# A two-layer decoder trunk: the first chunk fed from a transposed copy of x, and gate and up weights stored by chunk and row

## The reference, cut to what matters

```
def swiglu(x, w_gate, w_up, w_down):
    return (silu(x @ w_gate) * (x @ w_up)) @ w_down

for layer in range(2):
    x = x + 0.5 * swiglu(rmsnorm(x, ffn1_norm), ffn1_w_gate, ffn1_w_up, ffn1_w_down)
    h = rmsnorm(x, mix_norm)
    # h @ w_in gives q, k, v of three attention branches and three gate groups;
    # moba, sliding window with sinks, and differential attention with a headwise rmsnorm
    x = x + (sum of sigmoid(gate_i) * (branch_i @ P_i)) @ w_out
    x = x + 0.5 * swiglu(rmsnorm(x, ffn2_norm), ffn2_w_gate, ffn2_w_up, ffn2_w_down)
```

## Time and profile before

| | |
|---|---|
| time of the kernel, median of 3 runs | 1139.65 us (1139.65 to 1139.98) |
| time of the profiled execution | 1140.59 us |
| its span in the profile | 1138.8 us |
| PE busy | 1133.4 us |
| DVE busy | 770.4 us |
| ACT busy | 630.4 us |
| POOL busy | 70.3 us |
| read from memory | 205.29 MB |

### The profile page before, as it was taken

One profiled execution on the slowest core, in us unless ns is written; L12 is line 12 of the kernel. 1 busy time (PEld: TensorE's weight loads), 2 busy tenths in 40 slices (PEclk: granted clock), 3 DMA queues, 4 the chain that ended last, 5 costly groups with the idle time before them and its releaser, 6 DMA issues.

```text
span 1138.8 us, 16092 instructions
## 1 busy us (share of the span) xinstructions
PE 1133.4 (100%) x5975; PEld 966.9 (85%) x5975; DVE 770.4 (68%) x1055; ACT 630.4 (55%) x941; POOL 70.3 (6%) x79
## 2 busy tenths in 40 slices
PE   9999999999999999999999999999999999999999
PEld 7888888888888888888888888888888888888887
DVE  5766666868768676655766856678676695766655
ACT  6644455666684564544564544466666745544542
POOL 3020000202000000000020200002110000000000
PEclk9999999999999999999999999999999999999999
DMA  9955554545544665556566555636445445655521
GB/s 326 318 175 196 187 196 134 185 144 190 148 148 150 220 222 189 190 178 219 173 166 228 185 185 186 204 98 216 148 156 178 176 156 186 222 185 201 194 87 37
DMA packets 138828, 207.34 MB, mean 182 GB/s; under 512 B 6898, under 2 KB 99876, under 8 KB 138756
## 3 DMA queue, kind: packets, MB, share of 16 engines
q1 hardware_dynamic: 137364, 205.02, 54.5%
q0 software_dynamic: 752, 0.79, 0.7%
q10 hardware_dynamic: 640, 0.55, 0.2%
HBM read 205.29 MB, written 1.05 MB: 181 GB/s over the span
## 4 chain that ended last, share of the span: by engine, by line
PE 98%; ACT 1%; DVE 1%; issue 0%; DVEq 0%; ACTq 0%; POOL 0%; POOLq 0%
PE bank L560 28%; PE bank L530 16%; PE bank L534 16%; PE bank L533 16%; PE bank L564 15%; PE bank L546 1%; PE bank L859 1%; PE bank L849 1%; PE bank L830 1%; ACT probs L1202 1%; PE bank L848 1%; PE bank L877 1%; PE bank L668 0%; PE bank L569 0%; ACT w_high L1016 0%
## 5 line engine op out<-in xcount | busy, mean ns | idle before, releaser
L1300 DVE TENSOR_TENSOR w_low<-raw,w_high 128x1024 fp32r<-128x1024 f32 x388 | 464.2, 1232 | 282.1 <-ACT w_high L1016 281.4
L1016 ACT ACTIVATE w_high<-raw 128x1024 fp32r<-128x1024 f32 x387 | 393.6, 1055 | 318.4 <-PE bank L564 173.5
L560 PE MATMUL bank<-xT,w_high 128*128 128x512 f32 x1388 | 331.6, 390 | 0.1
L560 PEld LDWEIGHTS bank<-xT,w_high 128*128 128x128 f32 x1388 | 257.0, 188 | 51.2 <-DVE xT L1318 0.2
L564 PEld LDWEIGHTS bank<-xT,w_low 128*128 128x128 f32 x1408 | 175.7, 191 | 3.6
L564 PE MATMUL bank<-xT,w_low 128*128 128x256 f32 x1408 | 178.6, 283 | 0.0
L530 PE MATMUL bank<-w_high,xT 128*128 128x512 f32 (+1 forms) x440 | 171.3, 389 | 0.0
L534 PE MATMUL bank<-w_low,xT 128*128 128x512 f32 (+1 forms) x440 | 168.1, 382 | 0.0
L533 PE MATMUL bank<-w_high,xT 128*128 128x512 f32 (+1 forms) x440 | 168.1, 382 | 0.0
L530 PE MATMUL bank<-w_high,oT_high 128*128 128x512 f32 x418 | 162.6, 389 | 0.0
L534 PE MATMUL bank<-w_low,oT_high 128*128 128x512 f32 x418 | 162.2, 388 | 0.0
(11 more groups left out here) (146 smaller groups left out, 770.8 us busy)
## 6 DMA issues: line engine op xcount, KB each, us to landing
raw<-in_w_in SPq DMA_DIRECT2D x92, 512.0 KB, 4.5
raw<-in_ffn_w_down SPq DMA_DIRECT2D x88, 512.0 KB, 4.2
raw<-in_ffn_w_gate SPq DMA_DIRECT2D x86, 512.0 KB, 4.0
raw<-in_ffn_w_up SPq DMA_DIRECT2D x86, 512.0 KB, 5.0
raw<-in_w_out SPq DMA_DIRECT2D x16, 512.0 KB, 4.4
raw<-in_w_branch_c SPq DMA_DIRECT2D x8, 512.0 KB, 3.9
raw<-in_w_branch_a SPq DMA_DIRECT2D x4, 512.0 KB, 4.0
raw<-in_w_branch_b SPq DMA_DIRECT2D x4, 512.0 KB, 5.9
```

What stands on the lines that cost most here:

```text
L560: return nc.tensor.matmul(bank[b0 + n][:, :], w_high[:, slot, column(k, n)], xT[:, k], start=k == 0, stop=full_last and k == KB - 1)
L1016: act.activation(w_high[:, slot], raw[:, in_slot, (p % 2) * 1024:(p % 2) * 1024 + 1024], ACT.Copy).then_inc(sem["high_ready"], 1)
L1300: dve.tensor_tensor(w_low[:, slot], raw[:, FILL_SLOT[p // 2], (p % 2) * 1024:(p % 2) * 1024 + 1024], w_high[:, slot].bitcast(F32), ALU.sub ...
```

## The change

Three things are edited together.

1. **A transposed copy of x is an input.** The host passes `x_turned` (1024 x 256), `gains` (all gains and lam_init as columns, one transfer instead of four and some transposes), and x itself. The opening loads the transposed blocks in five pieces straight into SBUF (into the space of `o_nat`), so PE turns neither x nor the gains; ACT and DVE make the high and low blocks from SBUF. The first pair is split by its two row blocks: DVE itself copies the high half of block 0. ACT's squares of x are replaced by `sum_block_squares` on POOL, which squares the transposed x (two products of 128x1024) and adds the eight blocks together (sums of 1024, 512 and 256 columns); two matmuls with a column of ones (`sum_squares`) finish the sum over partitions. x in its normal layout is loaded later, by POOL's queue, and so are the parameters.
2. **Gate and up weights are laid out by chunk and row.** One array for gate and up together, so a fill of the ring is two transfers whose rows are 4 KB, and in the opening one transfer of 2 KB rows for each block, where both had 1 KB rows.
3. **Two numbers in the mixing part.** The first entries of `TURNS_AT` and `CONTEXTS_AT` go from 19 and 21 to 20 and 22.

On PE the turn of the norm's factor into a row (`turn_row`) moves: it stood between the wide passes of pairs 5 and 6, and stands after the narrow passes of pair 4; `sum_squares` takes its old place. The core of the diff:

```
-TURNS_AT = (19, 27, 35, 42)
-CONTEXTS_AT = (21, 29, 37, 44)
+TURNS_AT = (20, 27, 35, 42)
+CONTEXTS_AT = (22, 29, 37, 44)
...
-X_PIECES = (slice(0, 256), slice(256, 512), slice(512, 1024))
-WARM_FIRST, WARM_SECOND, WARM_THIRD = 6, 3, 6
+X_BLOCKS = ((0, 1), (1, 1), (2, 2), (4, 2), (6, 2))
+WARM = 11
...
+        def first_rows(engine, k0, nk, landed):
+            v = raw[:, FILL_SLOT[k0 // 4]].rearrange("p (k c) -> p k c", k=4)
+            for k in range(k0, k0 + nk):
+                engine.dma_start(v[:, k % 4], a["ffn1_gate_up"][0, 0, k // 4, :, k % 4]).then_inc(landed, 16)
...
+            def gate_up(w, layer, c, k0):
                 def sources(slot):
-                    v = slot.rearrange("p (k g c) -> p k g c", k=4, g=2)
-                    for g, w in enumerate((wg, wu)):
-                        yield v[:, :, g], w[bass.ds(layer, 1), k0 * P:(k0 + 4) * P, bass.ds(c * FC, FC)].rearrange(
-                            "o (k p) c -> p (o k) c", p=P)
+                    v = slot.rearrange("p (k c) -> p k c", k=4)
+                    for k in (0, 2):
+                        yield v[:, k:k + 2], w[bass.ds(layer, 1), bass.ds(c, 1), k0 // 4, :, k:k + 2].rearrange("o n p k c -> p (o n k) c")
...
+            load_x_turned(0)
+            load_x_turned(1)
+            load_x_turned(2)
+            first_rows(sp, 2, 2, fill_landed[FILL_SLOT[0]])
+            load_x_turned(3)
+            first_rows(sp, 4, 2, third_landed)
+            load_x_turned(4)
+            first_rows(sp, 6, 2, fill_landed[FILL_SLOT[1]])
...
+            def sum_block_squares():
+                for first, pieces in ((0, (0, 1, 2)), (D, (3, 4))):
+                    for piece in pieces:
+                        pool.wait_ge(x_turned_landed[piece], 16)
+                    v = x_turned[:, first:first + D]
+                    pool.tensor_tensor(x_squares[:, first:first + D], v, v, ALU.mult)
+                for width in (D, D // 2, D // 4):
+                    pool.drain()
+                    pool.tensor_tensor(x_squares[:, 0:width], x_squares[:, 0:width], x_squares[:, width:2 * width], ALU.add)
+                pool.drain().then_inc(block_squares_summed, 1)
...
+                pe.wait_ge(block0_high, 1)
                 pe.wait_ge(half_high, 1)
                 for n in range(4):
                     high_part(0, n, w_high, True)
+                pe.wait_ge(half_low, 1)
+                for n in range(4):
+                    high_part(0, n)
+                pe.wait_ge(block0_low, 1)
+                for n in range(4):
+                    low_part(0, n)
...
+            def cold_start():
+                act.wait_ge(gains_loaded, 16)
+                act.wait_ge(x_turned_landed[0], 16)
+                block(0).then_inc(block0_high, 1)
+                act.wait_ge(x_turned_landed[1], 16)
+                block(1).then_inc(sem["blocks_high"], 1)
                 high(0, 0)
+                for p in range(1, 4):
+                    act.wait_ge(x_turned_landed[p + 1], 16)
+                    block(2 * p)
+                    block(2 * p + 1).then_inc(sem["blocks_high"], 1)
+                    high(0, p)
                 high(0, 4)
...
+            def cold_pairs():
...
+                dve.wait_ge(half_landed[0], 16)
+                dve.tensor_copy(w_high[:, slot, 0:512], raw[:, in_slot, 0:512]).then_inc(half_high, 1)
+                dve.drain()
+                half_of_low(slice(0, 512)).then_inc(half_low, 1)
+                dve.wait_ge(block0_high, 1)
+                block_low(0).then_inc(block0_low, 1)
+                dve.wait_ge(sem["blocks_high"], 1)
+                block_low(1).then_inc(sem["blocks_low"], 1)
+                dve.wait_ge(sem["high_ready"], value("high_ready", 0, 1))
+                half_of_low(slice(512, 1024)).then_inc(sem["low_ready"], 1)
+                for p in range(1, 4):
+                    dve.wait_ge(sem["blocks_high"], p + 1)
+                    block_low(2 * p)
+                    block_low(2 * p + 1).then_inc(sem["blocks_low"], 1)
+                    low(0, p)
```

More of the change, by code:

```diff
@@ L506, in _ @@
                 pool.wait_ge(sem["hidden_ready"], value("hidden_ready", layer, 4))
+                if layer == 0:
+                    for half in range(HALVES):
+                        pool.dma_start(x[:, half], a["x"][0, half * P:half * P + P, :]).then_inc(x_loaded, 16)
                 pool.wait_ge(trig_loaded, 16)
@@ L667, in warm @@
                 for _ in range(count):
-                    nc.tensor.matmul(bank[7][:, :].rearrange("p (a b) -> p a b", a=4), zero[:, :],
-                                     zero[:, :].unsqueeze(1).to_broadcast([P, 4, P]), start=True, stop=True)
+                    nc.tensor.matmul(bank[7][:, :].rearrange("p (a b) -> p a b", a=4), ones[:, :],
+                                     ones[:, :].unsqueeze(1).to_broadcast([P, 4, P]), start=True, stop=True)
             def cold_chunk():
                 b0 = inner_bank(1)
[L675 to L680, removed]
                 full, high_part, low_part = inner_parts(PAIR_SLOT[0], b0)
-                pe.wait_ge(sem["blocks_high"], 1)
+                pe.wait_ge(block0_high, 1)
                 pe.wait_ge(half_high, 1)
@@ L688, in cold_chunk @@
                     high_part(1, n, w_high)
[L689 removed]
                 pe.wait_ge(sem["blocks_low"], 1)
[L691 to L693 removed]
+                for n in range(4):
+                    low_part(1, n)
                 pe.wait_ge(sem["low_ready"], value("low_ready", 0, 1))
[L695 to L697 removed]
+                for n in range(4):
+                    last = high_part(1, n)
                 last.then_inc(sem["pair_used"], 1)
@@ L716, in cold_chunk, with sum_squares @@
                     last.then_inc(sem["gate_up_done" if p == 3 else "pair_used"], 1)
-            def cold_row():
+            def sum_squares():
                 pe.wait_ge(sem["up_summed"], 1)
-                turn_row(0, 1, 4)
-                pe.wait_ge(rows_loaded, 16 * 3)
-                nc.tensor.transpose(bank[5][:, 0:GAIN_ROWS], gain_rows[0:GAIN_ROWS, :], ident[0:GAIN_ROWS, 0:GAIN_ROWS]).then_inc(gains_turned, 1)
+                pe.wait_ge(block_squares_summed, 1)
+                for half in range(HALVES):
+                    last = nc.tensor.matmul(bank[4][:, half:half + 1], x_squares[:, half * P:half * P + P], ones[:, 0:1].bitcast(F32),
+                                            start=True, stop=True)
+                last.then_inc(squares_summed, 1)
             def opening_proj_pair(layer):
@@ L782, in chunk @@
                     if opens and not turned:
-                        cold_row()
+                        sum_squares()
                     gate_up_wide(layer, p + 2, 2, done + 1, i * 12)
                     gate_up_narrow(layer, p, 0, done + 1, i * 12).then_inc(sem["pair_used"], 1)
+                    if opens and not turned:
+                        turn_row(0, 1, 4)
                     gate_up_narrow(layer, p + 1, 1, done + 1, i * 12).then_inc(sem["pair_used"], 1)
@@ L1642, in _ @@
             dve.sem_inc(sem["low_ready"], CREDIT["low_ready"])
-            dve.wait_ge(first_gains_ready, 1)
-            dve.wait_ge(lam_init_ready, 1)
             for layer in range(DEPTH):
                 if layer == 0:
-                    for p in range(4):
-                        blocks_low(layer, ST_FFN1, p // 2, G_FFN1, (p % 2,))
-                        low(layer, p)
+                    cold_pairs()
                 else:
@@ L1680, in rotary_constants, with gate_up_rows, gain_columns @@
     return np.ascontiguousarray(table.reshape(2, HALVES, P, DH).transpose(2, 0, 1, 3).astype(np.float32))
+def gate_up_rows(gate, up):
+    both = np.stack([gate, up], axis=2).reshape(DEPTH, 2, 4, P, 2, CHUNKS, FC)
+    return np.ascontiguousarray(both.transpose(0, 5, 1, 3, 2, 4, 6).reshape(DEPTH, CHUNKS, 2, P, 4, 2 * FC))
+def gain_columns(inputs):
+    columns = [inputs[name].reshape(DEPTH, KB, P).transpose(2, 0, 1) for name in ("ffn1_norm", "mix_norm", "ffn2_norm")]
+    columns.append(inputs["diff_subln"].reshape(DEPTH, 1, P).transpose(2, 0, 1))
+    columns.append(np.broadcast_to(np.asarray(LAM_INIT, np.float32).reshape(1, DEPTH, 1), (P, DEPTH, 1)))
+    return np.ascontiguousarray(np.concatenate(columns, axis=2).astype(np.float32))
 def kernel(**inputs):
@@ L1688 @@
     arrays = {name: np.ascontiguousarray(inputs[name]) for name in _INS}
+    arrays["x_turned"] = np.ascontiguousarray(inputs["x"][0].T)
+    arrays["gains"] = gain_columns(inputs)
+    for n in ("ffn1", "ffn2"):
+        arrays[f"{n}_gate_up"] = gate_up_rows(inputs[f"{n}_w_gate"], inputs[f"{n}_w_up"])
     arrays["trig"] = rotary_constants()
```

149 lines of the change are left out of this document (64 added, 85 removed).

## The result

The changed kernel takes 1143.17 us (median of 9 runs, 1142.00 to 1144.11), the kernel before 1140.02 (9 runs, 1139.65 to 1140.31). The ratio is 1.0026, with a 95% interval of 1.0018 to 1.0035: slower by about a quarter of a per cent. The spread is part of the story: before, nine runs lay within 0.7 us, after, within 2.1.

What follows compares the result with a forecast made beforehand. The prediction took PE to bound the kernel (busy 1133.4 of 1138.8 us). Opening +3.5, second chunk +1.3 and mixing part -1.8 gave +3.0, so 1142.5 us, range 1137.0 to 1145.2.

Steps and rivals of the forecast that it cites:

- What bounds the kernel: Whole kernel: PE bounds; only PE's work, its waits and the time before its first real matmul can move the time.
- The opening without POOL: Opening, POOL ignored: PE starts at 5.8 instead of 8.07, the stage ends at 18.1 against 21.02, gain 2.9.
- POOL and DVE in turns: Opening: SBUF instructions of POOL and DVE alternate whole, so the second chunk's first wide pass comes at 24.5, +3.5.
- The prediction's own lower price of 2.0: Opening: at 2.0 us per POOL product of 1024 columns, the stage ends at 23.0, +2.0.
- The second chunk: Second chunk: sum of squares 0.5, row turn 0.3, new wait 1.2, against 0.67 before: +1.3, from 0 to 1.9.
- The new wait for the hidden low part: Second chunk: the row turned later relative to PE's work makes PE wait 1.2 us for `hidden_low`.
- The mixing part: Mixing part: PE's wait for the probabilities in each layer goes, -1.8, from -1.5 to -1.9; 0 if it only moves.
- Transfers: After the opening: rows of 4 KB are worth nothing, since PE covers the transfers.
- The sum: Whole kernel: +3.5 + 1.3 - 1.8 = +3.0, giving 1142.5 us.
- (a): Opening: POOL and DVE don't hold each other up, or POOL takes under half the time; -3.4, 1136.2; chance 0.15.
- (b): Opening, second chunk: cheaper turns (2.0 a product, earlier transfers) or no wait for `hidden_low`; about +1.6, 1141.2; chance 0.2.
- (c): Opening: PE idles from 14.0 to 18.1 and its clock falls to half; +1.6, 1144.1; chance 0.1.

Runs made afterwards that it cites:

- the fifth: Kernel with squares on ACT, row early, DVE's sums ahead of its low parts, plus DVE waiting for the norm's factor before pair 7's low part: 1138.24 us, ratio 0.9981.
- after: The changed kernel itself, all three edits together, against the kernel before: 1143.17 us, ratio 1.0026.

## Why the prediction came out as it did

**What bounds the kernel.** Right. The chain is still PE for 97%. The list of what can move the time lacked one kind, though: PE doing the same work at half clock, which cost about 1 us in some executions.

**The opening without POOL.** Forecast 18.1, measured 18.53 to 18.64 in four kernels that keep POOL's products out of the way, and 19.04 in the fifth. In after PE started at 5.87, forecast 5.8, behind 11 matmuls that are on ones and not, as the forecast has it, on zeros. The pieces landed about as placed: ACT took weight block 1 at 7.46 and pairs 1, 2 and 3 at 9.20, 11.31 and 13.39, against 7.2, 8.6, 10.8 and 12.9.

**POOL and DVE in turns.** The mechanism was right and its size was not. Forecast 24.5 (+3.5), measured 23.33 (+2.31). The term at fault is the price of a product of 1024 columns: 2.45 us, scaled from broadcast products, where a plain one takes 1.89. (The sum of 512 columns took 1.29, forecast 1.25.) The prediction's own lower price of 2.0 gave 23.0, 0.3 too early. The products also began later (7.97, not 6.8), when DVE had already done blocks 0 and 1. The runs with memsets, with late products and with the products on ACT show the cause; the one with more products shows that its size follows POOL's work, though not one for one.

**The second chunk.** The new wait for the hidden low part was forecast at 1.2 and measured at 1.17; the sum of squares costs 0.36 of PE (26.98 to 27.34), forecast 0.5. In all +1.52 against +1.3. The parts that the trace names (0.36, 0.13 for the turn, 1.17) make 1.7 of the 2.2 us by which this chunk is longer than a plain one; the rest is not accounted for. A further 0.23 comes in the third chunk, which the prediction did not have: one of its first wide passes waits 0.3 us for DVE's up sum of the chunk before, which comes after four subtractions that start at 36.36, late like the hidden low part.

**The mixing part.** Forecast -1.8. Measured between the traces -1.9, by single edits -1.6 to -2.1.

**Transfers.** Right: worth nothing after the opening (ratio 1.0004 alone).

**The sum.** +2.31 + 1.52 + 0.23 - 1.9 = +2.2 between the traces, forecast +3.0. The medians stand 3.1 apart, which looks like the forecast of 3.0 and is partly luck: POOL's turns were put 1.2 us too dear, and that was made up by the offset of 1.0 between profiled runs and medians, to which the half clock of some executions, in no term of the sum, adds its part. In the time itself the forecast stood on the median of three runs, 1139.65, where nine give 1140.02.

**The rivals.** (a) fell with the first look at DVE's 2.29 us. (b), turns but cheaper ones, at 2.0 us a product, had a chance of 0.2 and came true in its first condition: a product took 1.89, and the opening lost 2.31 where (b) has 2.0. Between the traces the whole loss of 2.2 lies in the middle between (b)'s 1.6 and the forecast's 3.0. Its second condition, that the wait for the hidden low part doesn't appear, did not come. (c) was given a chance of 0.1 as a case of its own. It is real, but it is no case that excludes the forecast: it comes to some executions of the same kernel and not to others, and costs about 1 us there (the second chunk begins at 24.43 or, with the numbers taken back, at 24.12 instead of 23.33), not 1.6.

## What to carry to other kernels

Before a job is moved to an idle engine, look at what it reads and who reads there at the same time: POOL was idle 94% of the time, yet each of its instructions that reads SBUF holds up a DVE instruction with two SBUF inputs for the whole of its length, and the other way round. Look for neighbours of that kind in the trace of before; two of them at 72 us told the whole case. And measure the parts of a change one by one: one part here gained 2 us, one was worth nothing, and one cost 4 to 5 (4.1 between the traces, 4.7 by the medians with the two numbers taken back).

## What the runs showed that was not expected

- POOL and DVE take strict turns even when one of them works on two columns: 0.19 us becomes 1.01, 0.73 becomes 1.52.
- A memset of 128x2048 on POOL takes 1.8 us and does not hold DVE up at all.
- From 13 to 16.5 us the opening of after streamed at 410 GB/s (DMA share 1.03) with rows of 2 and 4 KB, against 348 before with rows of 1 KB (share 1.10). The layout of the weights alone, all else as before, gives 394 (share 1.01).
- Behind a wait of PE of 2.6 us the clock fell to half in some executions and not in others. The spread of the kernel's times was 2.1 us with it, and 0.8 with the wait filled.
